# Differential attention: where the band's value weights are split and multiplied, and how its heads are normed

## The chip, the cores and the metric
The kernel runs on one core of a Trainium2 chip. The metric is the device time of one execution in microseconds. It was timed three times; the median counts.

## The reference, cut to what matters
One block of a network on 512 tokens of width 1024: layer norm, a mixer of two attentions with gates, a mixture of 32 experts, and a second block of the same kind. The change touches the first mixer alone.

```python
def diff_attention(q, k, v, lam, lam_init, subln_w):      # 4 heads, two score maps each, values of width 128
    ...
        p = jax.nn.softmax(jnp.where(allowed, s + bias, -jnp.inf), axis=-1)
        a = p[0] - lam * p[1]
        return jnp.einsum('bhqk,bhkd->bhqd', a.astype(v.dtype), v)
    ...
    o = rms_norm(o, subln_w) * (1.0 - lam_init)
    return o.reshape(B, S, WIDTH_A)

    out_a = diff_attention(qa, ka, va, lam, lam_init, subln_w)
    out_b = chunk_band_attention(qb, kb, vb, rel_bias)
    merged = gates[:, :, 0] * (out_a @ w_branch_a) + gates[:, :, 1] * (out_b @ w_branch_b)
```
All of `qa` to `vb` are columns of `h @ w_in`. `rms_norm` works over the 128 values of one head.

## The kernel before, in words
The program is a list of stages. In a stage each engine has its own instructions and the engines meet by counting semaphores; at a stage's end all engines meet (a border). 512 tokens are 4 rows of 128 partitions (`NT`), the width of 1024 is 8 tiles of 128 (`NK`). Every product with weights is made of three TensorE products of 32-bit operands (`split_product`, lines 137 to 139): the weights are cast to an upper part (`fp32r`) by ScalarE, and `split_lower` (line 144) subtracts it from the raw weights on VectorE or GpSimd.

The stages around the change:
- `opening_stage` norms the input, makes the differential values and the projections of the first unit.
- `diff_heads` (`heads_stage`, 4 units of 4 items, numbered t = 0 to 15). An item is 128 queries against 128, 256, 384 or 512 keys. In step t TensorE makes the scores of item t and a piece of the next unit's projections (`projection`; units 2 and 3 are split inside the stage, GpSimd making the lower parts), then turns the weights of item t−2 (`TURN_LAG`) and multiplies values for item t−3 (`VALUE_LAG`). VectorE adds the bias of item t (line 649), and scales item t−1 (lines 680 to 686); ScalarE copies the turned weights of item t−2 out of PSUM (line 720) and takes the exponentials of item t (line 736). The last unit projects nothing. When a unit closes, VectorE copies its 128 columns to `oa` (line 3480). Steps 16 to 18 only finish the last items. SP (the DMA queue) loads the weights of a unit when the projections of an earlier one are done, and with `following` (`band_values`) loads the band's 2 MB of value weights into `ahead` once all projections are done.
- `diffnorm` (`transpose_heads_stage`) does two things at once. The heads: VectorE squares all of `oa` (line 1065), sums (1072), ScalarE takes the root (1108), VectorE the reciprocal (1080) and scales all of `oa` in one operation (1084); TensorE turns it by 16 transposes (1140), ScalarE copies each of the four tiles out of PSUM with the weight column (1114), and VectorE casts and splits each (1090, 144). The band's values for rows 0 and 1 of 4: ScalarE casts the weights by four parts (1105), VectorE makes four lower parts (144), and TensorE multiplies 48 products, 36 ahead of the transposes and 12 behind them; ScalarE copies the two banks out (1120). SP loads the weight column and the band's bias table.
- `bandbias` is a stage of one memset on VectorE (line 761), after the table has landed.
- `band_heads` (`heads_stage` again): SP loads its first weights, TensorE makes 48 products for value rows 2 and 3, then the projections of the first unit, then items as above.

Then come the merge, the output, the routing and the experts, none of which the change touches. Loads of later stages are issued when a semaphore of earlier work allows it.

Of the kernel before, what the change touches and what calls it, by code (L numbers as in the profile page):

```python
# [16 lines left out]
P = 128  # L17
# [554 lines left out]
def attention_pe(nc, pe, k, items, b, projection, opened):  # L572

    N, at = items.n, b["at"]
    for t in range(N + VALUE_LAG):
        if t < N:
# [13 lines left out]
            if not items.closes(t):  # L590
                projection(u + 1, items.place(t))
        n = t - TURN_LAG
# [41 lines left out]
def attention_dve(nc, dve, k, items, b, next_keys, copy_out, ordered, other):  # L634

    N, at = items.n, b["at"]
    for t in range(N + VALUE_LAG + 1):
# [59 lines left out]
        if t < N:  # L697
            other(items.unit(t), items.place(t))
        n = t - VALUE_LAG
        if 0 <= n < N and items.closes(n):  # L700
# [4 lines left out]
            copy_out(u).then_inc(b["out_copied"], 2 if items.mixed else 1)  # L705


def attention_act(nc, act, k, items, b, weights, next_queries, copy_out):

    N, at = items.n, b["at"]  # L710
    for t in range(N + VALUE_LAG + 1):
# [15 lines left out]
        if t < N:  # L727
# [11 lines left out]
            weights(items.unit(t) + 2, items.place(t))  # L739
        n = t - VALUE_LAG  # L740
# [12 lines left out]
def band_bias_stage(nc, k, table):  # L753

    with Stage(nc, "bandbias") as st:
        block = st.block()

        @block.vector
        def _(dve):
            dve.wait_ge(k.band_table_in, 16)  # L760
            nc.vector.memset(table[0:HD, :, S - HD:S], NEG)
# [12 lines left out]

def heads_stage(nc, name, k, load, projections, items, values, q, copy_out, upper_out=None, keys=None, following=None,
                projected_values=False, first=None, beside=None,
                opened=False, prepare=None):
# [4 lines left out]
    with Stage(nc, name) as st:  # L782
# [39 lines left out]
        def _(sp):  # L822
            for u in range(split, units):
# [21 lines left out]
        def _(pe):  # L845
# [42 lines left out]
            attention_pe(nc, pe, k, items, b, projection, opened)  # L888

        @block.scalar  # L890
        def _(act):
# [5 lines left out]

            def weights(u, step):
                if beside is not None and u == 2 and step == 0:
                    upper_part(1, 0)  # L900
# [37 lines left out]
            attention_act(nc, act, k, items, b, weights, next_queries, upper_out)  # L938

        @block.vector  # L940
        def _(dve):
# [20 lines left out]

            def remainders(u, step):
                if beside is not None and u >= 1 and step in (3, 5):
# [5 lines left out]
            attention_dve(nc, dve, k, items, b, next_keys, copy_out, keys is not None and upper_out is not None, remainders)  # L970
# [4 lines left out]
                    v_hi=NT if early else 0, v_ps=len(v_rows), v_sb=len(v_rows))  # L975
# [41 lines left out]
def transpose_heads_stage(nc, name, k, o, o_t, heads=0, weight=None, eps=LN_EPS, factor=1.0, ahead=None, values=None,  # L1017
                          next_upper=None):

    width = o.shape[2]
    tiles = width // P
    n, t0 = k.heads.done["ready"], k.heads.done["transposed"]
    with Stage(nc, name) as st:
# [2606 lines left out]
```

## Time and profile before

| | us |
|---|---|
| median of 3 runs | 2034.96 (2034.91 to 2036.11) |
| profiled execution, its own time | 2034.65 |
| its span | 2032.8 |
| mean granted TensorE clock | 0.981 of full speed |
| TensorE busy | 1933.8 (95%) |
| VectorE busy | 1574.0 (77%) |
| ScalarE busy | 1231.0 (61%) |
| GpSimd busy | 296.8 (15%) |

The differential stage runs from 60 to 130 us of the span, the norm stage to 150, the band from 151. In the rows a line is start, duration, engine, line of the kernel, operation, output<-inputs with shapes; in square brackets stands the engine's idle time before it and what ended it. PE is TensorE, DVE VectorE, ACT ScalarE, POOL GpSimd, SP the DMA queue; "PEq L83" is the border of a stage. Where neighbouring instructions overlap, the distance from start to start is the pace. PEclk is the granted clock of TensorE, 1.00 for 2.4 GHz and 0.50 for 1.2 GHz.

### The profile page before, as it was taken

Reading aid. Unit: us, or ns where it says so; the run is one execution under the profiler, and the core shown is the slowest. Engines: PE = TensorE matmul, PEld = TensorE weight load, DVE = VectorE, ACT = ScalarE, POOL = GpSimd, SP = SyncE. Lnnn points to the kernel's source line nnn. Section 1 sums busy time; section 2 is a strip of 40 time slices with the busy share of each in tenths; the row PEclk is TensorE's granted clock in tenths of the full one; section 3 lists DMA queues with packets and bytes.
Section 4 is the critical chain, followed back from the end, with each engine's and each line's share of the span. In section 5 each row is a group of like instructions: output and inputs, shape, how many; then the busy total and the mean of one; then the engine's idle time right before and its main releaser. Section 6 shows DMA issues by size and latency. Waiting matters only on the chain. (4 is left out here: it accounts for less than half of the span.)

```text
span 2032.8 us, 28745 instructions
## 1 busy us (share of the span) xinstructions
PE 1933.8 (95%) x10074; PEld 1550.4 (76%) x10074; DVE 1574.0 (77%) x1778; ACT 1231.0 (61%) x1319; POOL 296.8 (15%) x172
## 2 busy tenths in 40 slices
PE   6979899989999999999999999999999898899898
PEld 5657678766888888888888888888888685587776
DVE  6662451479999999999999999999999865754787
ACT  3443522326777777777777777777777534753551
POOL 0102044101112111111211121111212100000100
PEclk9989999998999999999999999999999998999999
DMA  6223133539999999999999999999999752011222
GB/s 212 69 84 83 43 98 98 181 135 372 353 392 378 395 374 393 385 384 393 377 392 375 393 384 385 387 382 390 378 396 373 255 110 76 17 37 63 63 65 82
DMA packets 201788, 518.44 MB, mean 255 GB/s; under 512 B 22118, under 2 KB 81678, under 8 KB 201372
## 3 DMA queue, kind: packets, MB, share of 16 engines
q1 hardware_dynamic: 191532, 482.70, 63.9%
q0 software_dynamic: 9360, 34.08, 6.4%
q8 instruction: 41, 0.67, 0.1%
q10 hardware_dynamic: 832, 0.80, 0.1%
q14 instruction: 23, 0.19, 0.0%
HBM read 494.43 MB, written 28.88 MB: 257 GB/s over the span
## 5 line engine op out<-in xcount | busy, mean ns | idle before, releaser
L1991 PE MATMUL bank<-moe_upper,x_hi 128*128 128x512 f32 x1504 | 603.4, 401 | 0.0
L1993 PE MATMUL bank<-moe_upper,x_hi 128*128 128x512 f32 x1504 | 585.9, 390 | 0.0
L2212 DVE TENSOR_TENSOR beyond_lower<-beyond,moe_upper 128x2048 fp32r<-128x2048 f32 x192 | 434.7, 2285 | 32.4 <-ACT moe_upper L2114 32.4
L2114 ACT CAST moe_upper<-beyond 128x2048 fp32r<-128x2048 f32 x192 | 367.6, 1915 | 141.4 <-PE bank L1993 136.8
L1991 PEld LDWEIGHTS bank<-moe_upper,x_hi 128*128 128x128 f32 x1504 | 282.8, 188 | 62.4 <-issue 0.3
L1993 PEld LDWEIGHTS bank<-moe_upper,x_hi 128*128 128x128 f32 x1504 | 282.3, 188 | 59.7
L1992 PE MATMUL bank<-beyond_lower,x_hi 128*128 128x512 f32 x752 | 293.0, 390 | 0.0
L2212 DVE TENSOR_TENSOR mixed_t_lower<-mixed_t,moe_upper 128x2048 fp32r<-128x2048 f32 x96 | 218.2, 2286 | 27.0 <-ACT moe_upper L2114 26.9
L2114 ACT CAST moe_upper<-above 128x2048 fp32r<-128x2048 f32 x96 | 183.6, 1914 | 72.9 <-PE bank L1993 72.9
L2212 DVE TENSOR_TENSOR above_lower<-above,moe_upper 128x2048 fp32r<-128x2048 f32 x96 | 218.1, 2285 | 6.3 <-ACT moe_upper L2114 6.3
L2114 ACT CAST moe_upper<-mixed_t 128x2048 fp32r<-128x2048 f32 x96 | 183.8, 1916 | 58.0 <-PE bank L1993 56.1
L1992 PEld LDWEIGHTS bank<-beyond_lower,x_hi 128*128 128x128 f32 x752 | 141.4, 188 | 28.1
L1992 PE MATMUL bank<-mixed_t_lower,x_hi 128*128 128x512 f32 x376 | 146.8, 390 | 0.0
L1992 PE MATMUL bank<-above_lower,x_hi 128*128 128x512 f32 x376 | 146.3, 389 | 0.0
L1939 POOL COPY moe_dst<-row 128x1 uint32 (+1 forms) x31 | 26.6, 858 | 596.0 <-ACT y L2103 596.0
L139 PE MATMUL bank<-x_hi,ahead_lower 128*128 128x512 f32 x264 | 103.1, 391 | 0.0
L1941 POOL DMA_INDIRECT mixed<-y,moe_dst x31 | 85.0, 2742 | 26.7 <-issue 26.7
L1992 PEld LDWEIGHTS bank<-above_lower,x_hi 128*128 128x128 f32 x376 | 70.6, 188 | 14.6
L1992 PEld LDWEIGHTS bank<-mixed_t_lower,x_hi 128*128 128x128 f32 x376 | 70.9, 188 | 13.5
L1283 DVE TENSOR_TENSOR merge_tmp<-merge_sig,bank 128x512 f32<-128x512 f32 x8 | 5.5, 687 | 81.0 <-PE bank L139 80.6
L1931 POOL COPY moe_tok<-token 128x1 uint32 (+1 forms) x32 | 24.8, 775 | 288.2 <-DMA mixed<-y,moe_dst 268.7
L1933 POOL DMA_INDIRECT ahead<-h,moe_tok x32 | 58.0, 1813 | 26.9 <-issue 26.9
(632 smaller groups left out, 3413.5 us busy)
## 6 DMA issues: line engine op xcount, KB each, us to landing
beyond<-in_w_exp_in_dram SPq DMA_DIRECT2D x128, 1024.0 KB, 8.1
mixed_t<-in_w_exp_in_dram SPq DMA_DIRECT2D x64, 1024.0 KB, 8.1
above<-in_w_exp_in_dram SPq DMA_DIRECT2D x64, 1024.0 KB, 8.1
beyond<-in_w_exp_out_dram SPq DMA_DIRECT2D x64, 1024.0 KB, 9.5
mixed_t<-in_w_exp_out_dram SPq DMA_DIRECT2D x32, 1024.0 KB, 7.6
above<-in_w_exp_out_dram SPq DMA_DIRECT2D x32, 1024.0 KB, 9.4
ahead<-in_w_in_dram SPq DMA_DIRECT2D x23, 512.0 KB, 5.4
ahead<-in_w_in_dram SPq DMA_DIRECT2D x3, 1536.0 KB, 6.7
```

The lines of the kernel that those rows point to most:

```text
L139: return nc.tensor.matmul(out, lhs.lo, rhs.hi, start=False, stop=stop)
L1283: nc.vector.tensor_tensor(tmp[:, :], sig[:, 0, :], k.bank[2][:, :], ALU.mult)
L1931: nc.gpsimd.tensor_copy(tok[:, p:p + 1], r.token[:, ds(j, 1)])
L1933: nc.gpsimd.indirect_dma_start(out=rows_in[p][:, :], out_offset=None, in_=k.h1[:, :], in_offset=bass.IndirectOffsetOnAxis(ap=tok[:, p:p + ...
L1939: nc.gpsimd.tensor_copy(dst[:, :], r.row[:, ds(j, 1)])
L1941: nc.gpsimd.indirect_dma_start(out=k.mixed[:, :], out_offset=bass.IndirectOffsetOnAxis(ap=dst[:, 0:1], axis=0), in_=y[:, :], in_offset=Non ...
L1991: nc.tensor.matmul(to, hi[:, f, :], upper[u][:, t, cols], start=f == 0 and not biased, stop=False)
L1992: nc.tensor.matmul(to, hi[:, f, :], lower[s][:, t, cols], start=False, stop=False)
L1993: done = nc.tensor.matmul(to, lo[:, f, :], upper[u][:, t, cols], start=False, stop=f == NK - 1)
L2114: nc.scalar.copy(upper[h % SPLIT][:, :, :], ring[s][:, :, :]).then_inc(hi_ready, 1)
L2212: nc.vector.tensor_tensor(lower[s][:, :, :], ring[s][:, :, :], upper[h % SPLIT][:, :, :].bitcast(F32), ALU.subtract).then_inc(lo_ready, 1)
```

## The change
- The band's value weights are loaded in two halves of 1 MB: tiles 4 to 7 at the start of `diff_heads`, ahead of unit 2's weights, and tiles 0 to 3 where all 2 MB were loaded before. The weight column is loaded behind them, in `diff_heads`.
- Inside `diff_heads`: ScalarE casts all four parts (2 and 3 in units 0 and 1, 0 behind the last item's exponentials, 1 in step 16), VectorE makes lower parts 2 and 3 (units 0 and 1) and 0 (step 16), and TensorE makes the 24 products of tiles 4 to 7 in steps 12, 13, 14, 16 and 17 (`LATER_STEPS`: six, three, three, six, six), into banks 7 and 0.
- VectorE squares and sums a unit's head right after its copy to `oa`; for the third unit in step 16.
- The new `differential_norm_stage` scales the heads by quarters, and TensorE turns each quarter when it is scaled; it makes 12 products ahead of the transposes and 12 behind them, with lower part 1 made there.
- The stage `bandbias` is gone: its memset and a drain come behind the first key copy of `band_heads`.

```diff
@@ attention_pe
+        if spare is not None:
+            spare(t - N + items.per_unit)
         n = t - TURN_LAG
@@ attention_dve
         if t < N:
             other(items.unit(t), items.place(t))
+        elif spare is not None:
+            spare(t - N)
...
             copy_out(u).then_inc(b["out_copied"], 2 if items.mixed else 1)
+            if summed is not None and u != items.units - 2:
+                summed(u)
@@ attention_act
             weights(items.unit(t) + 2, items.place(t))
+        elif spare is not None:
+            spare(t - N)
@@
-def band_bias_stage(nc, k, table):
...
+def band_bias(nc, k, table, dve):
+
+    dve.wait_ge(k.band_table_in, 16)
+    nc.vector.memset(table[0:HD, :, S - HD:S], NEG)
+    dve.drain()
@@
+LATER_BANKS, LATER_ORDER = (7, 0), (2, 3, 0, 1)
+LATER_STEPS = {0: ((0, 4), (0, 5)), 1: ((0, 6),), 2: ((0, 7),), 4: ((1, 4), (1, 5)), 5: ((1, 6), (1, 7))}
+
+
+def load_later(sp, k, weights, half):
+
+    part = slice(NK // 2 * half, NK // 2 * half + NK // 2)
+    sp.dma_start(k.ahead[:, part, :], weights[:, part, :]).then_inc(k.ahead_in, 16)
+    k.ahead_loads += 16
@@ heads_stage
         @block.sync
         def _(sp):
+            if later is not None:
+                load_later(sp, k, later.weights, 1)
             for u in range(split, units):
...
-            attention_pe(nc, pe, k, items, b, projection, opened)
+
+            def later_products(step):
+                if step == 4:
+                    pe.wait_ge(b["biased"], b["at"] + items.n - 1)
+                for i, c in LATER_STEPS.get(step, ()):
+                    if c % 2 == 0:
+                        pe.wait_ge(v_lo, v0 + c // 2 - 1)
+                    split_product(nc, k.bank[LATER_BANKS[i]][:, :], k.x_parts[:, c, i * P:(i + 1) * P], v_w[:, c, :],
+                                  c == NK // 2, False)
...
+            def later_upper(h):
+                if h == 2:
+                    act.wait_ge(k.ahead_in, ahead_loads + 16)
+                elif h == 0:
+                    act.wait_ge(k.ahead_in, ahead_loads + 32)
+                part = slice(2 * h, 2 * h + 2)
+                nc.scalar.copy(v_upper[:, part, :], k.ahead[:, part, :]).then_inc(v_hi, 1)
+
+            def last_upper(step):
+                if step == 0:
+                    later_upper(1)
+
             def weights(u, step):
+                if later is not None and u in (2, 3) and step == 1:
+                    later_upper(u)
+                if later is not None and u == units + 1 and step == STEPS - 1:
+                    later_upper(0)
...
+            def squares(u):
+                part = later.heads[:, :, u * P:u * P + P]
+                dve.drain()
+                nc.vector.tensor_tensor(later.squares, part, part, ALU.mult)
+                dve.drain()
+                nc.vector.tensor_reduce(later.sums[:, :, u], later.squares, AX.X, ALU.add)
+
+            def last_lower(step):
+                if step == 0:
+                    squares(units - 2)
+                    later_lower(0)
+
             def remainders(u, step):
+                if later is not None and u < 2 and step == 2:
+                    later_lower(u + 2)
@@ differential_norm_stage, in place of transpose_heads_stage
         @block.sync
         def _(sp):
+            ahead(sp)
 
         @block.vector
         def _(dve):
+            nc.vector.tensor_scalar(sums[:, :, :], sums[:, :, :], 1.0 / P, LN_EPS, ALU.mult, ALU.add).then_inc(sum_ready, 1)
+            dve.wait_ge(weight_in, 16)
+            nc.vector.tensor_scalar(wcol[:, :], wcol[:, :], 1.0 - LAM_INIT, None, ALU.mult).then_inc(weight_ready, 1)
+            split_lower(nc.vector, k.ahead[:, 2:4, :], k.v_upper[:, 2:4, :], v_w.lo[:, 2:4, :]).then_inc(v_lo, 1)
+            dve.wait_ge(std_ready, 1)
+            nc.vector.reciprocal(sums[:, :, :], std[:, :, :])
+            dve.drain()
+            for c in range(NT):
+                part = o[:, :, c * P:c * P + P]
+                nc.vector.tensor_tensor(part, part, sums[:, :, c].unsqueeze(2).to_broadcast([P, NT, P]), ALU.mult)\
+                    .then_inc(scaled if c < NT - 1 else ready, 1)
+            for c in range(NT):
+                dve.wait_ge(tile_out, c + 1)
+                nc.vector.tensor_copy(o_t.hi[:, c, :], out[:, c, :])
                 dve.drain()
+                split_lower(nc.vector, out[:, c, :], o_t.hi[:, c, :], o_t.lo[:, c, :])
...
         @block.tensor
         def _(pe):
+            def value_products(i, h):
+                for c in (2 * h, 2 * h + 1):
+                    last = split_product(nc, k.bank[LATER_BANKS[i]][:, :], k.x_parts[:, c, i * P:(i + 1) * P],
+                                         v_w[:, c, :], False, c == NK // 2 - 1)
+                return last
+
+            pe.wait_ge(v_lo, lo0 + 3)
+            for i in range(2):
+                value_products(i, 0)
+            for c in range(NT):
+                if c < NT - 1:
+                    pe.wait_ge(scaled, c + 1)
+                else:
+                    pe.wait_ge(ready, 1)
                 for i in range(NT):
...
+            pe.wait_ge(v_lo, lo0 + 4)
+            for i in range(2):
+                value_products(i, 1).then_inc(v_ps, 1)
@@ program
             def band_values(sp):
-                load_ahead(sp, k, column_tiles(A["w_in"][0], 5 * WA, 512))
+                load_later(sp, k, later.weights, 0)
+                with nc.allow_non_contiguous_dma(reason="a column of weights"):
+                    sp.dma_start(later.wcol[:, :], A["subln_w"].rearrange("o p -> p o")).then_inc(k.heads["weight_in"], 16)
...
-            band_bias_stage(nc, k, band_table)
...
-                lambda m: None, band_lower, band_upper, following=merge_early, projected_values=True)
+                lambda m: None, band_lower, band_upper, following=merge_early, projected_values=True,
+                prepare=lambda dve: band_bias(nc, k, band_table, dve))
```

## Rows read from the trace of the kernel before
**Rows 1.** The page of the profile, its first line.
```profile
span 2032.8 us, 28745 instructions
```

**Rows 2.** Busy time by stage: window, its length, busy time of each engine, clock, DMA.
```profile
60.00:110.90 50.90, 49.89 (x251) 36.82 (x251) 28.00 (x92) 21.65 (x61) 9.44 (x4) 1.00 0.21 62
110.90:129.20 18.30, 13.77 (x80) 9.66 (x79) 12.97 (x46) 9.24 (x27) 0.00 (x0) 0.91 0.33 116
129.20:133.77 4.57, 0.00 (x0) 0.00 (x0) 4.17 (x4) 3.50 (x4) 0.00 (x0) 0.71 0.43 102
133.77:144.01 10.24, 10.24 (x37) 8.22 (x37) 8.32 (x8) 1.88 (x3) 0.00 (x0) 0.80 0.42 159
...
148.70:151.15 2.45, 0.00 (x0) 0.03 (x1) 1.64 (x4) 0.58 (x1) 0.00 (x0) 1.00 0.00 0
151.15:163.76 12.61, 12.61 (x49) 10.26 (x49) 0.00 (x0) 2.48 (x3) 4.75 (x2) 0.86 0.32 84
```

**Rows 3.** The timeline of VectorE, 129 to 151 us.
```profile
129.28 0.69 DVE L3480 COPY oa<-bank 128x512 f32<-128x512 f32 x1 [3.19 <-PE bank L623]
130.29 2.29 DVE L1065 TENSOR_TENSOR diffnorm_sq<-oa 128x2048 f32<-128x2048 f32 x1 [0.32 <-PEq L83]
132.50 2.35 DVE L144 TENSOR_TENSOR ahead_lower<-ahead,v_upper 128x1024 fp32r<-128x1024 f32 x2
...
135.01 2.29 DVE L1072 TENSOR_REDUCE diffnorm_sums<-diffnorm_sq 128x16 f32<-128x2048 f32 x1
...
138.59 0.24 DVE L1080 RECIPROCAL diffnorm_sums<-diffnorm_std 128x16 f32<-128x16 f32 x1
...
145.43 0.43 DVE L1090 CAST oa_t_upper<-oa_t 128x512 fp32r<-128x512 f32 x1 [3.09 <-ACT oa_t L1114]
...
149.24 0.69 DVE L144 TENSOR_TENSOR oa_t_lower<-oa_t,oa_t_upper 128x512 fp32r<-128x512 f32 x1
...
150.36 0.48 DVE L761 MEMSET band_table<- 64x512 f32 x1 [0.43 <-PEq L83]
```

**Rows 4.** The timeline of ScalarE: a table load, a cast, the evictions.
```profile
11.22 1.28 ACT L187 ACT_TABLE_LOAD   x1
12.51 0.20 ACT L187 ACTIVATE setup_std<-setup_ve 128x4 f32<-128x4 f32 x1
...
73.30 1.04 ACT L896 CAST first_upper<-first_raw 128x1024 fp32r<-128x1024 f32 x1
...
144.70 2.42 ACT L1114 ACTIVATE oa_t<-bank,diffnorm_wcol 128x512 f32<-128x512 f32 x4 [6.91 <-PE bank L1140]
```

**Rows 5.** The timeline of TensorE, 143 to 152 us.
```profile
143.78 0.39 PE L139 MATMUL bank<-v_upper,x_lo 128*128 128x512 f32 x1
144.01 1.91 PE L1140 MATMUL bank<-const,oa 128*128 128x128 f32 x16
...
151.15 0.47 PE L137 MATMUL bank<-v_upper,x_hi 128*128 128x512 f32 x1 [2.47 <-PEq L83]
```

**Rows 6.** The timeline of TensorE in the last unit of the differential stage.
```profile
114.71 0.55 PE L601 MATMUL bank<-const,diff_scores 128*128 128x128 f32 x3 [1.73 <-DVE diff_scores L686]
...
124.28 0.90 PE L601 MATMUL bank<-const,diff_scores 128*128 128x128 f32 x3 [2.00 <-DVE diff_scores L686]
124.97 1.06 PE L623 MATMUL bank<-v,diff_pt 128*128 128x128 f32 x4
126.15 1.11 PE L601 MATMUL bank<-const,diff_scores 128*128 128x128 f32 x4
```

**Rows 7.** The timeline of VectorE and GpSimd, 79 and 115 us.
```profile
79.53 2.95 DVE L686 SCALAR_TENSOR_TENSOR diff_scores<-diff_scores,diff_l 128x512 f32<-128x512 f32 x1
79.57 2.36 POOL L144 TENSOR_TENSOR first_raw_lower<-first_raw,first_upper 128x1024 fp32r<-128x1024 f32 x1 [2.80 <-ACT first_upper L896]
...
115.86 0.75 DVE L686 SCALAR_TENSOR_TENSOR diff_scores<-diff_scores,diff_l 128x512 f32<-128x512 f32 x1
```

**Rows 8.** DMA issues, 55 to 72 us: count, KB each, us to landing.
```profile
first_raw<-in_w_in_dram SPq DMA_DIRECT2D x2, 512.0 KB, 6.7
```

More of the change, by code:

```diff
@@ L937, in _ @@
                     upper_part(1, n)
-            attention_act(nc, act, k, items, b, weights, next_queries, upper_out)
+            attention_act(nc, act, k, items, b, weights, next_queries, upper_out, None if later is None else last_upper)
         @block.vector
@@ L968, in remainders @@
                     split_lower(nc.vector, k.ahead[:, :, part], beside[:, :, part], k.ahead_lower[:, :, part])
-            attention_dve(nc, dve, k, items, b, next_keys, copy_out, keys is not None and upper_out is not None, remainders)
+            attention_dve(nc, dve, k, items, b, next_keys, copy_out, keys is not None and upper_out is not None, remainders,
+                          None if later is None else squares, None if later is None else last_lower)
     k.attention.counted(scored=items.n, out_copied=2 * units)
@@ L1044, in _ @@
         def _(sp):
-            if heads:
-                with nc.allow_non_contiguous_dma(reason="a column of weights"):
-                    sp.dma_start(wcol[:, :], weight).then_inc(weight_in, 16)
-            if ahead is not None:
-                ahead(sp)
+            ahead(sp)
         @block.vector
         def _(dve):
-            if next_upper is not None:
-                for m in range(4):
-                    part = slice(P * m, P * m + P)
-                    dve.wait_ge(next_hi, m + 1)
-                    split_lower(nc.vector, k.ahead[:, :, part], next_upper[:, :, part], k.ahead_lower[:, :, part])
@@ L1117, in _ @@
-            if values is not None:
-                for i in range(2):
-                    act.wait_ge(v_ps, i + 1)
-                    nc.scalar.copy(values[:, i, :], k.bank[4 + i][:, :])
+            act.wait_ge(sum_ready, 1)
+            nc.scalar.activation(std[:, :, :], sums[:, :, :], ACT.Sqrt).then_inc(std_ready, 1)
+            act.wait_ge(weight_ready, 1)
+            for c in range(NT):
+                act.wait_ge(transposed, c + 1)
+                nc.scalar.activation(out[:, c, :], k.bank[NORM_TURNED + c][:, :], ACT.Copy, scale=wcol[:, 0:1])\
+                    .then_inc(tile_out, 1)
@@ L1141, in _ @@
                 last.then_inc(transposed, 1)
-            if values is not None:
-                value_products(3)
-    k.heads.counted(transposed=tiles, ready=1 if heads else 0)
+            pe.wait_ge(v_lo, lo0 + 4)
+            for i in range(2):
+                value_products(i, 1).then_inc(v_ps, 1)
+    k.units.counted(v_lo=1)
+    k.heads.counted(transposed=NT, ready=1)
 def load_merge(sp, w_in, branches, raw, f, loaded):
@@ L3476, in program @@
                 first = first_raw, first_lower, first_upper
+                later = Kernel()
+                later.weights, later.heads = column_tiles(A["w_in"][0], 5 * WA, 512), oa[:, :, :]
+                later.sums = s2.enter_context(nc.sbuf_tensor("head_sums", [P, NT, NT], F32))[:, :, :]
+                later.squares = oa_t.whole[:, 0, :].rearrange("p (i d) -> p i d", d=P)
+                later.wcol = s2.enter_context(nc.sbuf_tensor("head_weight", [P, 1], F32))
                 opening_stage(nc, k, A, table, first)
```

135 lines of the change are left out of this document (31 added, 104 removed).

## Prediction, made before the changed kernel ran

> **What bounds the kernel now.** I read first the span [rows 1]; the profiled execution took 2034.65 us, 1.85 us more than it, and the median of the three runs is 2034.96 us, 0.31 us above. So what I take off the span comes off both, and the median stands 0.31 us above the profiled one. Then I cut the stretch around the change by stage and asked for busy time and clock [rows 2]. Three things are to be seen. Up to 110.9 us TensorE is busy 49.9 of 50.9 us: it is the bound, and VectorE (28.0) and ScalarE (21.7) have room. From 110.9 to 129.2 us, the last unit of differential attention, nobody is full: TensorE 13.8 of 18.3 us, a chain that goes round the engines. Then TensorE does nothing for 4.57 us, works 10.24 us at a granted clock of 0.80, and after the stage does nothing for 2.45 us; the 48 products that open the band stage take 12.61 us at 0.86.
>
> Third, the timeline of each engine there. VectorE's [rows 3] shows the norm stage as a staircase: the last `oa` copy at 129.28, squares, two `lower` parts, the sums, the scaling, and from 145.43 to 149.93 four casts with their remainders, then a stage for one memset at 150.36. TensorE's [rows 5] shows the transposes at 144.01, behind 36 products, and the band at 151.15. From VectorE's first instruction of the norm stage to TensorE's first of the band it is 151.15 − 130.29 = 20.86 us.
>
> **The norm stage, after.** I count from its first VectorE instruction, T, at which TensorE begins too.
> - ScalarE: table load 1.28 and square root 0.20 [rows 4], with nothing ahead of them now (the four casts are gone): 1.5 us.
> - VectorE: the two small operations (0.08 apart, 0.3 with the issue) and one `lower` part (2.35 for two, 1.2 each) [rows 3]: also 1.5. The reciprocal with its gap, 0.3–0.4 [rows 3], to 1.9. Four quarter scalings at the price of a 128x512 tensor_tensor, 0.69, some 0.61 from start to start [rows 3]: the first is ready at 2.6, the last at 4.45.
> - TensorE: 12 products before the transposes instead of 36, at 0.23 each (143.78 to 144.01 [rows 5]) 2.75, so the first transpose starts at 2.85, just after the first quarter is scaled.
> - From first transpose to first cast passed 144.01 to 145.43, 1.42 [rows 3, 5]: 4.3; VectorE is free at 4.45. So the casts start at 4.45, and they took 4.5 us for all four: 8.95. TensorE's other 12 products end at about 7.5 and their evictions (0.6 each, as the four of 2.42 [rows 4]) at about 8.5, beside them.
> - One border, 0.32 (129.97 to 130.29 [rows 3]), and no stage for the memset: TensorE starts the band at 9.3.
>
> Gain: 20.86 − 9.3 = **11.55 us**. The memset of 0.48 us moves behind VectorE's key copy in the band. The first scores wait on TensorE for that copy too, and the second item's come microseconds of projections later; if the cover were gone it would cost 0.5. I take 0.
>
> **What goes into the differential stage.** Each piece, and what hides it:
> - 24 products move to the last unit. At 0.23 us, the six at its first item (1.4) fit the 1.73 us in which TensorE waited before 114.71, and the six of step 4 (1.4) fit the 2.00 us before 124.28 [rows 6]. The three and three between have 0.3 us of idle: they push the next scores, which VectorE (13.0 of 18.3 us busy [rows 2]) takes up in part. I book 0.4, about half of the 0.7 that three products last. The last six come directly ahead of the last item's transposes (126.15), a chain without idle: 1.4 us. Against it, the stretch from 124.28 ran at the lower level (0.91 for the unit as a whole [rows 2]); with the idle filled I expect 2.4 GHz, by which the 3 transposes and 4 value products (124.28 to 126.03) take 0.9 instead of 1.75, and the rest up to the copy some 0.5 less. So: 0.4 + 1.4 − 0.85 − 0.5, about 0.4 us on `oa`'s last copy. Bounds: nothing, and 3.1 if the clock stays low and the six take twice as long.
> - Head squares and sums. A pair costs 0.69 and 0.65 (a quarter of the 2.29 of the reduction [rows 3], with its overhead) and drains: 1.4. Units 0 and 1 have it while TensorE projects; unit 2's comes with `lower` 0 (1.2) after VectorE's last scaling (the transposes that wait for it start at 126.15 [rows 6]), 2.6 us in the 3.19 us that it idles before 129.28 [rows 3]. Unit 3's has no cover: the stage ends with it, **1.4 us**. Bounds 1.2 and 1.6.
> - `lower` parts 2 and 3 on VectorE, four casts of 1.04 on ScalarE [rows 4]: the first two on either engine in units 0 and 1, where TensorE is the bound. The last two casts lie behind the last exponentials and between the last copies of transposed scores: TensorE is behind its six products by then. 0.
> - SP: half the value weights (1 MB) now go ahead of unit 2's weights, and the rest behind the projections, 1 MB instead of 2. Unit 2's two landed 6.7 us after their issue at 60.06 [rows 8], and are cast at 73.30 [rows 4]: 6.5 us of slack. Another 1 MB, at what these two took, is 6.7 at the very most; I expect it hidden, bounds 0 and 0.5. The weight column is loaded earlier; the band's table is issued first in the norm stage and is needed at the memset, over 20 us on.
>
> So the differential stage ends 1.8 us later (at 131.8 against 129.97).
>
> **The band's start.** TensorE stood still 2.45 us before 151.15, and the products behind ran at 0.86 [rows 2]. 48 at 0.23 are 10.95 us, against 12.61: 1.65 us lost to the lower level. After the change TensorE ends its products at T + 7.5 and goes on at T + 9.3: 1.8 us, or less. Rows of the same unit: 1.73 us idle before 114.71 was followed by products of unchanged pace, 2.00 before 124.28 by slower ones [rows 6]. 1.8 lies between, nearer 1.73: I take the clock as kept, **−1.65 us**; the other bound is 0.
>
> **Sum.** 2034.65 − 11.55 + 1.8 − 1.65 = 2023.25 us; on the median of the runs, **2023.6 us**. Behind the band's start each piece is shifted alike, since its loads are issued by progress, not by time.
>
> **Two rules against the trace.** ScalarE's table load at 11.22 is followed by an activation at 12.51, 1.29 us on [rows 4]: nothing is lost beyond the load's 1.28. The Trainium skill, "ScalarE: Activation LUTs", What ACT_TABLE_LOAD costs, gives a switch 1283 ns plus a drain of about 1380 ns. The rule would put the square root, and with it all of VectorE's staircase, 1.3 us later; the trace of before does not agree with it. VectorE's 128x512 scalar_tensor_tensor at 79.53 took 2.95 us, begun as GpSimd's split of 2.36 us ran; at 115.86, with GpSimd idle, it took 0.75 [rows 7]. The Trainium skill, "SBUF — State Buffer", on the shared port pair, has it that an operation with two SBUF inputs and one of GpSimd exclude each other for the whole instruction; the trace agrees with that, and the new squares and `lower` parts are such operations.
>
> **Rivals.**
> - *The clock falls.* TensorE idles about 2.5 us before T (4.57 before less the 3.48 that it waited inside the stage, and the 1.4 of the sums), and 2.00 and 2.45 us were followed by the lower level. The 10.24 us at 0.80 hold 4.1 us at the lower level, in which only nine of the 36 products fit [rows 2], 0.45 each. Most of the 12 products at that, 5.1 in all: the transposes start at 5.2 and the stage lasts 11.6: 2.3 us lost; with the band's start low too, 1.65 more; with the tail at its bound, 2.7 more. 2025.9, 2027.6 or 2030.3 us. For it: the gap is in the range that brought it. Against: the tail, now denser, counts beside it. 0.30.
> - *The table switch costs more than its row*, by 1.3: the scalings end at 5.75 and the casts with them: 2024.9 us. 0.04.
> - *VectorE collides with GpSimd* in the differential stage: 2.2 us each time (2.95 − 0.75). There are seven new two-input operations there (four squares, three `lower` parts); the splits are four, and TensorE's projections cover units 0 and 1. All seven on the path would cost 15.4, to 2039.0 us, slower. It decides from the seventh collision on; before it only eats the gain. 0.02.
> - *The gain is given back*, by a load or a clock further down: within 0.2%, above 2030.9 us. 0.04.
> - *More is gained*, below 2021.8 us: the tail wholly hidden and a quarter of a stage besides. 0.05.
> - The forecast, 2021.8 to 2025 us: 0.55.
>
> **Range and chances.** About 0.2% (4.1 us) is what a measurement of this kernel can tell from no change. The low end is the sum with the tail's 1.8 hidden; the high end is the clock rival without its last term and with a microsecond more: 2021.8 to 2028.6. Faster 0.94, within 0.2% 0.04, slower 0.02.
>
> **What would show it.** In the profile after: six products each in the gaps before the transposes of the 11th and the 15th of the sixteen items; the last `oa` copy within a microsecond of 129.3; squares and a sum after it; a norm stage of about 9 us with the first transpose 2.9 us in, VectorE without a wait from the scalings to the last remainder; clock 1.00 in it and in the band's first 11 us. Wrong would be: a clock of 0.5 there, TensorE waiting for ScalarE's casts in the tail, or a late table load.

## The result, and the profile after

The changed kernel takes 2022.49 us (median of 4 runs, 2020.8 to 2025.76) against 2034.93 us: a ratio of 0.9936, 95% interval 0.9916 to 0.9956, and 12.4 us less. The forecast was 2023.6 us, in a range of 2021.8 to 2028.6. The profiled execution took 2023.78 us, 10.9 below that of the kernel before. So the total came out as forecast; the stretch around the change did not quite, and that is what the rest is about.

The stages once more, cut at the same events as in [rows 2] (columns as there):
```profile
60.00:110.70 50.70, 49.89 (x251) 36.84 (x251) 32.94 (x98) 23.40 (x63) 9.45 (x4) 1.00 0.28 83
110.70:129.35 18.65, 17.64 (x103) 12.43 (x103) 15.59 (x49) 10.93 (x29) 0.00 (x0) 1.00 0.19 57
129.35:132.03 2.68, 0.03 (x1) 0.03 (x1) 2.07 (x3) 0.04 (x1) 0.00 (x0) 0.82 0.00 0
132.03:137.28 5.25, 5.25 (x12) 4.04 (x13) 4.11 (x8) 1.47 (x2) 0.00 (x0) 0.50 0.79 265
...
142.24:143.80 1.56, 0.00 (x0) 0.03 (x1) 1.19 (x3) 0.59 (x1) 0.00 (x0) 1.00 0.00 0
143.80:154.80 11.00, 11.00 (x48) 9.09 (x49) 0.00 (x0) 2.48 (x3) 3.37 (x2) 1.00 0.36 98
```
The last unit of the differential stage is now nearly full of TensorE work, 17.6 of 18.7 us (13.8 of 18.3 before), at a clock of 1.00 instead of 0.91, and it is only 0.35 us longer. Where 36 products took 10.24 us ahead of the transposes, there are now 12, but these take 5.25 us, since the clock is at 0.50 for all of them. The band's first 48 products run at 1.00 and take 11.00 us instead of 12.61.

VectorE, as in [rows 3]:
```profile
126.58 0.69 DVE L1014 TENSOR_TENSOR oa_t<-oa 128x512 f32<-128x512 f32 x1
127.34 0.69 DVE L1016 TENSOR_REDUCE head_sums<-oa_t 128x4 f32<-128x512 f32 x1
127.95 1.22 DVE L144 TENSOR_TENSOR ahead_lower<-ahead,v_upper 128x1024 fp32r<-128x1024 f32 x1
129.49 0.69 DVE L3501 COPY oa<-bank 128x512 f32<-128x512 f32 x1 [0.33 <-PE bank L625]
130.27 0.69 DVE L1014 TENSOR_TENSOR oa_t<-oa 128x512 f32<-128x512 f32 x1
131.04 0.69 DVE L1016 TENSOR_REDUCE head_sums<-oa_t 128x4 f32<-128x512 f32 x1
132.03 0.18 DVE L1104 TENSOR_SCALAR head_sums<-head_sums 128x16 f32<-128x16 f32 x1 [0.30 <-PEq L83]
...
133.87 2.50 DVE L1113 TENSOR_TENSOR oa<-oa,head_sums 128x512 f32<-128x512 f32 x4
139.00 0.43 DVE L1117 CAST oa_t_upper<-oa_t 128x512 fp32r<-128x512 f32 x1 [2.63 <-ACT oa_t L1128]
...
142.81 0.69 DVE L144 TENSOR_TENSOR oa_t_lower<-oa_t,oa_t_upper 128x512 fp32r<-128x512 f32 x1
```
The square, the sum and the `lower` part at 126.58 stand in what was an idle stretch; the last copy to `oa` starts at 129.49 (129.28 before); the square and the sum behind it, to 131.73, stand alone. The norm stage begins at 132.03. The four quarter scalings are over at 136.4, and then VectorE waits 2.63 us for the first turned tile, which the forecast had ready when VectorE was free. The remainders end at 143.50, and TensorE's next line shows the band 0.30 us later.

TensorE, as in [rows 5] and [rows 6]:
```profile
124.66 0.55 PE L603 MATMUL bank<-const,diff_scores 128*128 128x128 f32 x3 [0.78 <-DVE diff_scores L688]
...
126.87 0.60 PE L603 MATMUL bank<-const,diff_scores 128*128 128x128 f32 x4
...
132.03 0.77 PE L137 MATMUL bank<-v_upper,x_hi 128*128 128x512 f32 x1 [2.65 <-PEq L83]
132.59 0.63 PE L138 MATMUL bank<-ahead_lower,x_hi 128*128 128x512 f32 x1
133.02 0.63 PE L139 MATMUL bank<-v_upper,x_lo 128*128 128x512 f32 x1
...
137.28 2.20 PE L1151 MATMUL bank<-const,oa 128*128 128x128 f32 x16
...
143.80 0.47 PE L137 MATMUL bank<-v_upper,x_hi 128*128 128x512 f32 x1 [1.57 <-PEq L83]
```
The gap before the 15th item's transposes is 0.78 instead of 2.00 us: six products fill it, and 124.66 runs at the full pace (0.55 for the three transposes that took 0.90). TensorE then stands still for 2.65 us ahead of 132.03, and the products behind are 0.43 us apart (132.59 to 133.02) instead of 0.23. Ahead of 143.80 it stands still for 1.57 us, and what follows is at the full pace.

ScalarE's table load, as in [rows 4]:
```profile
132.00 1.28 ACT L1124 ACT_TABLE_LOAD   x1 [3.82 <-PEq L83]
133.29 0.22 ACT L1124 ACTIVATE diffnorm_std<-head_sums 128x16 f32<-128x16 f32 x1
```
The root follows 1.29 us behind the load's start. The drain of about 1.38 us that the Trainium skill, "ScalarE: Activation LUTs", What ACT_TABLE_LOAD costs, adds to each load does not show here either.

### The profile page after: what moved, and what is told of

Same layout as the page of the kernel before. It is cut to its first block and busy times, and to the rows that moved or that the text cites. A ratio compares the mean times of both kernels' runs of the same rounds, so it can differ in the third digit from the quotient of the medians.

```text
span 2022.0 us, 28752 instructions
## 1 busy us (share of the span) xinstructions
PE 1930.3 (95%) x10074; PEld 1546.7 (76%) x10074; DVE 1576.5 (78%) x1787; ACT 1230.7 (61%) x1319; POOL 291.1 (14%) x172
## 5 line engine op out<-in xcount | busy, mean ns | idle before, releaser
L139 PEld LDWEIGHTS bank<-x_hi,ahead_lower 128*128 128x128 f32 x264 | 49.6, 188 | 10.8
```

The costliest lines, as they stand in the source:

```text
L139: return nc.tensor.matmul(out, lhs.lo, rhs.hi, start=False, stop=stop)
```

## The experiments

Run times scatter more than the edits are worth: on the chips of the experiments the kernel before itself ran from 2030.4 to 2043.8 us. So each run is read on one stretch of its trace, from the differential stage's last key copy to the band's first, which every kernel has in the same places. The two rows that bound it in the changed kernel:
```profile
110.71 0.69 DVE L989 COPY diff_heads_kt<-bank 128x512 f32<-128x512 f32 x1 [0.45 <-PE bank L139]
...
165.88 0.69 DVE L989 COPY band_heads_kt<-bank 128x512 f32<-128x512 f32 x1 [10.19 <-PE bank L139]
```
The same differences for all, in us (T is VectorE's first instruction of the norm stage; the last column is the stretch between the two key copies; each is worked out from the starts in that kernel's timelines):

| kernel | key copy to T | T to first transpose | T to the band's first product | its 48 products | key copy to key copy |
|---|---|---|---|---|---|
| before | 19.35 | 13.72 | 20.86 | 12.61 | 63.90 |
| changed | 21.32 | 5.25 | 11.77 | 11.00 | 55.17 |
| after_again | 21.31 | 5.26 | 11.76 | 11.00 | 55.15 |
| after_third | 21.32 | 4.42 | 10.65 | 10.98 | 54.03 |
| fill_gap | 21.50 | 2.84 | 9.06 | 11.00 | 52.64 |
| early_products | 21.83 | 2.59 | 9.98 | 10.98 | 53.87 |
| early_fill | 21.83 | 2.58 | 9.05 | 11.00 | 52.96 |
| six_last | 21.04 | 2.81 | 9.05 | 11.00 | 52.16 |
| six_last_again | 21.05 | 2.82 | 9.05 | 10.96 | 52.14 |
| whole_scaling | 21.32 | 4.41 | 10.63 | 11.00 | 54.03 |
| sums_in_norm | 19.78 | 7.08 | 15.14 | 10.98 | 56.98 |
| products_in_norm | 20.96 | 9.65 | 15.87 | 11.00 | 58.91 |
| bias_inside | 19.36 | 13.83 | 20.06 | 11.00 | 61.50 |
| before_fill | 19.46 | 11.78 | 18.91 | 11.00 | 60.45 |

**The changed kernel again, twice** (no edit).

> The changed kernel once more, for a second trace and a fair spread. Theory (the gap sets the clock): TensorE's still time of about 2.6 us ahead of the norm stage is followed by the lower level, so the 12 products take about 5.1 us and the first transpose starts 5.2 us into the stage, as in the first trace; where the lower level ends may differ, and with it the runs scatter by 2 to 3 us, which those of the kernel before (1.5 us) do less. Rival (the products are slow for another reason, such as the 2 MB table load beside them): they take 5.1 us in every trace at a granted clock of 1.00. About 2022.5 us.

> The changed kernel a third time, as the neighbour of the next one. By the two traces so far the stretch from the last key copy of the differential stage to the first of the band is 55.2 us (63.9 in the kernel before), of which 2.5 us are the 12 products at the lower level. Theory: 55.2 again, or 52.6 where the lower level should miss them; the whole scatters by 2 us or more with the clock of other stretches.

2021.49 us (2019.67 to 2026.47) and 2023.85 us (2020.52 to 2027.91); ratios to the kernel before 0.9941 (0.9922 to 0.9959) and 0.9943 (0.9921 to 0.9964). The second trace repeats the first within 0.02 us; in the third the lower level came a little later and left sooner, 1.1 us better. So the 12 products are slow in each of the three traces, by an amount that varies with where the lower level begins and ends. The expectation that the kernel before scatters less was wrong: beside these runs it went from 2030.42 to 2040.38.

**fill_gap**: TensorE is given something to do in the gap.
```diff
             attention_pe(nc, pe, k, items, b, projection, opened, None if later is None else later_products)
+            if later is not None:
+                fill(nc, k, 5, 11)      # 11 products of x_hi with itself into bank 5, which nobody reads
```


> The changed kernel with 11 more products of no use on TensorE at the end of the differential stage, 0.23 us each, so that it is busy to the border. Theory (the gap sets the clock): the granted clock stays 1.00 through the norm stage, the 12 products take 2.75 us instead of 5.2, the first transpose starts at 2.9 us, the first cast is set by VectorE at 4.45 us, and the band starts 9.3 us into the stage instead of 11.8: 2.3 to 2.5 us less, about 2020 us, with less scatter. Rival (another reason): the 12 products keep 0.43 us each and the time stays at 2022.5 us. Second rival (the 11 products delay the border): up to 0.3 us of the gain is lost.

TensorE's timeline (line 156 is the filler):
```profile
129.31 2.78 PE L156 MATMUL bank<-x_hi 128*128 128x512 f32 x11
132.39 0.47 PE L137 MATMUL bank<-v_upper,x_hi 128*128 128x512 f32 x1 [0.30 <-PEq L83]
132.70 0.39 PE L138 MATMUL bank<-ahead_lower,x_hi 128*128 128x512 f32 x1
132.93 0.40 PE L139 MATMUL bank<-v_upper,x_lo 128*128 128x512 f32 x1
...
135.24 2.20 PE L1159 MATMUL bank<-const,oa 128*128 128x128 f32 x16
```
The gap is 0.30 us, the products are 0.23 us apart, and the first transpose starts 2.84 us in. The stage is 2.7 us shorter, the border 0.2 later: 52.64 us against 55.17. The table of the band's bias is loaded beside it as before, so it was not that. The stretch thus takes 11.26 us less than in the kernel before, against the forecast's sum of 11.4. The whole shows none of it: 2023.87 us (ratio 0.9944, 0.9927 to 0.9961) against its neighbour after_again's 2021.49, where about 2020 was expected. Its trace has more of the lower level elsewhere than that of after_again (from 1880 to 1920 us the clock is 0.87 against 1.00), and 2.5 us are less than the scatter.

**early_products and early_fill**: the 12 products ahead of the transposes go into the gap themselves; then fillers where the norm stage waits for its first quarter.
```diff
             attention_pe(nc, pe, k, items, b, projection, opened, None if later is None else later_products)
+            if later is not None:
+                pe.wait_ge(v_lo, v0 + 3)
+                for i in range(2):
+                    for c in (0, 1):
+                        split_product(...)
@@ differential_norm_stage
-            pe.wait_ge(v_lo, lo0 + 3)
-            for i in range(2):
-                value_products(i, 0)
+            fill(nc, k, 6, 9)           # early_fill only
```


> The changed kernel with the 12 products of tiles 0 and 1 moved from the start of the norm stage to the end of the differential one, where TensorE stands still. Theory (TensorE's 12 products at the lower level are what the norm stage waits for): the first transpose starts when the first quarter is scaled, 2.6 us into the stage, the casts follow VectorE's scalings at about 4.5 us, and the band starts 9.3 to 10 us in, whatever the clock; the differential stage ends up to 0.5 us later. 1.5 to 2.3 us below the changed kernel. Rival (ScalarE's or VectorE's staircase is the bound): no change beyond 0.5 us.

> The same, with 9 products of no use on TensorE at the start of the norm stage, where it would wait for the first quarter (2.1 us). Theory: the clock stays at 1.00 to the band's end of value products; the norm stage is VectorE's staircase, 9.3 us; against the kernel without these 9 it wins 0 to 1 us, where its last 12 products or the band's first ones ran at the lower level. Rival: the nine delay the transposes, up to 0.2 us lost.

2024.76 us (0.9952, 0.9934 to 0.9971) and 2024.51 us (0.9952, 0.9934 to 0.9969). The first transpose starts at 2.59 and 2.58 us, when the first quarter is scaled, and the border comes 0.5 us later, both as expected. The gain of early_products is less than expected: its stretch is 1.3 us shorter than the changed kernel's, not 1.5 to 2.3, because TensorE waits 2.88 us for the quarter instead, and the lower level comes there. Its TensorE timeline:
```profile
132.87 0.39 PE L139 MATMUL bank<-v_upper,x_lo 128*128 128x512 f32 x1
136.15 3.42 PE L1154 MATMUL bank<-const,oa 128*128 128x128 f32 x16 [2.88 <-DVE oa L1119]
139.22 0.78 PE L137 MATMUL bank<-v_upper,x_hi 128*128 128x512 f32 x1
```
The transposes take 3.42 us instead of 2.20, the last 12 products end late and their evictions set the end, 9.98 us in. With fillers it is 9.05. The gap had only been moved; of the two, 53.87 and 52.96 us, the second gains 2.2 over the changed kernel and pays 0.5 for the border.

**whole_scaling**: one scaling of all heads instead of four quarters.
```diff
-            for c in range(NT):
-                part = o[:, :, c * P:c * P + P]
-                nc.vector.tensor_tensor(part, part, sums[:, :, c]..., ALU.mult).then_inc(scaled if c < NT - 1 else ready, 1)
+            nc.vector.tensor_tensor(o3, o3, r3, ALU.mult).then_inc(ready, 1)
```


> The changed kernel with the heads scaled by one operation and turned after it, as before. Theory (the 12 products at the lower level end at 5.2 us, so the quarters are ready long before they are used): the scaled heads are ready at 4.2 us instead of a first quarter at 2.6, and nothing moves, 0 to 0.2 us, as long as the clock is low; with a full clock it would cost 1.3 us. Rival (the quarters bring what the norm stage gained): 1.5 us or more longer.

2023.41 us (0.9919, 0.9896 to 0.9943). Its row in the table is that of after_third, which had the lower level in the same place, to 0.02 us: the first transpose at 4.41 and 4.42. The quarters brought nothing there, since the 12 products end later than the whole scaling. That they would bring 1.3 us at a full clock was not measured by itself; fill_gap, with quarters, starts its transposes 2.84 us in, 1.3 us before the 4.12 at which the whole scaling ends here.

**sums_in_norm**: squares and sums of all heads in the norm stage.
```diff
+            nc.vector.tensor_tensor(later.squares, o, o, ALU.mult)
+            dve.drain()
+            nc.vector.tensor_reduce(sums[:, :, :], later.squares..., AX.X, ALU.add)
```


> The changed kernel with squares and sums of all heads back in the norm stage, 2.29 us each. Theory: the differential stage ends 1.4 us earlier, and VectorE's first quarter is scaled at 6.9 us instead of 2.6, so the casts start at about 8.8 instead of 7.0 us (they waited for TensorE): 1.8 minus 1.4, about 0.4 us longer than the changed kernel at a low clock, 2.9 against one at a full clock. Rival (the sums by pair are a gain by themselves): 3 us or more longer.

2027.56 us (0.9942, 0.992 to 0.9964), stretch 56.98. The differential stage ends 1.54 us earlier, the first quarter and the first cast (9.01 us in) come as expected, and yet it is 1.8 us longer than the changed kernel, not 0.4. TensorE, with nothing to do for 4.09 us, was at the lower level for the transposes and the first few of the last products, as its timeline has it:
```profile
138.64 3.67 PE L1147 MATMUL bank<-const,oa 128*128 128x128 f32 x16 [4.09 <-DVE oa L1109]
141.96 0.78 PE L137 MATMUL bank<-v_upper,x_hi 128*128 128x512 f32 x1
...
146.70 0.47 PE L137 MATMUL bank<-v_upper,x_hi 128*128 128x512 f32 x1 [0.92 <-PEq L83]
```
Its evictions then end the stage, 15.14 us in, and not VectorE's remainders at 13.5. So the sums by pair were worth 1.8 us against the first two traces of the changed kernel and 2.95 against the third; how much of it is the clock was not taken apart.

**products_in_norm**: all 48 value products in the norm stage, casts and lower parts where the change put them.
```diff
-            attention_pe(..., opened, None if later is None else later_products)
+            attention_pe(..., opened)
@@ differential_norm_stage
-            pe.wait_ge(v_lo, lo0 + 3)
-            for i in range(2):
-                value_products(i, 0)
+            for h in (2, 3, 0):
+                pe.wait_ge(v_lo, lo0 + (h - 1 if h else 3))
+                for i in range(2):
+                    value_products(i, h)
```


> The changed kernel with all 48 value products in the norm stage; casts and lower parts stay in the differential stage. Theory (TensorE's products are the norm stage's bound): 36 products ahead of the transposes, 8.2 us at the full clock and up to 11 with 5 us at the lower one, so the first transpose at 9 to 11 us instead of 5.2 and the band 3.5 to 5.5 us later within the stage; the differential stage ends 0.4 to 0.5 us earlier. 3 to 5 us longer than the changed kernel. Rival (it was the casts' absence that brought the gain, TensorE's share is hidden): below 2 us longer.

2028.96 us (0.9956, 0.9936 to 0.9977), stretch 58.91: 3.7 us longer, with the first transpose at 9.65 us and the border 0.36 earlier. The 24 moved products are worth 3.7 of the 8.7 us of the stretch, net of the 0.4 that they cost where they went, the largest of the parts undone here. The clock has a share in that too: the 36 products ahead of the transposes ran at the lower level for their first 3 us, the changed kernel's 12 for all 5.25. What it is worth to have ScalarE's four casts out of the norm stage was not measured by itself.

**six_last, twice**: the last six of the moved products behind the last item's value products.
```diff
-LATER_STEPS = {..., 4: ((1, 4), (1, 5)), 5: ((1, 6), (1, 7))}
+LATER_STEPS = {..., 4: ((1, 4), (1, 5)), 7: ((1, 6), (1, 7))}
...
             attention_pe(nc, pe, k, items, b, projection, opened, None if later is None else later_products)
+            if later is not None:
+                later_products(7)
```


> The changed kernel with the last six products inside the differential stage moved from ahead of the last item's transposes to behind its value products. Theory (they stand in a chain without idle): the last copy to oa starts 0.4 to 0.8 us earlier, and so does the norm stage; and TensorE stands still 1.2 us before it instead of 2.6, so the lower level may stay away, 2.3 us more. Between 0.5 and 3 us below the changed kernel. Rival (the six kept the clock up in the tail): the tail falls to the lower level and the last copy is no earlier.

> The kernel with the last six products behind the last item's value products, once more. Theory: the same stretch takes 52.2 us, 3.0 less than the changed kernel (0.3 by the earlier copy, 2.7 by the clock), in this trace too, since TensorE stands still only 1.2 us. Whether the whole time shows it: 0 to 3 us less than its neighbour. Rival (the full clock of the first trace was luck): 54 to 55 us in this one.

TensorE in the second, first its timeline:
```profile
125.12 0.55 PE L603 MATMUL bank<-const,diff_scores 128*128 128x128 f32 x3 [0.77 <-DVE diff_scores L688]
...
127.00 0.66 PE L603 MATMUL bank<-const,diff_scores 128*128 128x128 f32 x4 [0.89 <-DVE diff_scores L688]
...
129.32 0.48 PE L137 MATMUL bank<-v_upper,x_hi 128*128 128x512 f32 x1
```
and its busy time by window (the clock is the third number from the right):
```profile
126.00:129.00 3.00, 2.03 (x17) 1.73 (x16) 2.76 (x5) 2.13 (x4) 0.00 (x0) 1.00 0.00 0
...
130.70:132.20 1.50, 0.27 (x2) 0.02 (x1) 1.14 (x2) 0.02 (x1) 0.00 (x0) 1.00 0.00 0
132.20:141.20 9.00, 7.78 (x40) 6.07 (x40) 8.24 (x16) 5.07 (x8) 0.00 (x0) 1.00 0.68 233
```
Nothing stands between value products and the transposes at 127.00 now, which wait 0.89 us for VectorE: the six had cost the chain 0.28 us, less than the 0.4 expected, because VectorE was the later one. Behind 129.32 stand the six, the gap is 1.25 us (1.5 of the window at 130.7), and the clock is 1.00 throughout. 52.16 and 52.14 us in two traces, 3.0 less than the changed kernel and the best of all. The runs took 2022.62 us (0.9929, 0.9902 to 0.9955) and 2021.18 us (0.9933, 0.9912 to 0.9955). All 10 have a median of 2021.6, all 16 of the changed kernel of 2022.8; an advantage of 1.2 us that these runs do not establish.

**bias_inside and before_fill**, on the kernel before: the memset's stage alone taken away; TensorE's gap of 4.57 us filled.
```diff
-            band_bias_stage(nc, k, band_table)
...
+                prepare=lambda dve: band_bias(nc, k, band_table, dve))
```
```diff
             attention_pe(nc, pe, k, items, b, projection, opened)
+            if opened_early:            # the differential stage
+                fill(nc, k, 5, 4)
@@ transpose_heads_stage
             if values is not None:
+                fill(nc, k, 6, 14)
```


> The kernel before with one edit of the change: the stage of the memset is gone and the memset stands behind the band's first key copy. Theory: one border and the memset, 1.22 us from the last remainder to TensorE's first product, become 0.31: 0.9 us less, and the first scores' bias is not later. Rival (the memset shows in the band): nothing gained.

> The kernel before with 4 products of no use at the end of the differential stage and 14 at the start of the norm stage, where TensorE stands still for 4.57 us. Theory (the gap sets the clock): the 36 products ahead of the transposes run at 0.23 us from about 133.8 us on and take 8.3 us instead of 10.2, so the transposes start at 142.1 instead of 144.0 us: 1.9 us less. Rival (contention with the table load, not the clock): the 36 products still take 10.2 us.

2034.12 us (0.9992, 0.9979 to 1.0006) and 2035.43 us (0.9996, 0.9983 to 1.001), neither apart from the kernel before, whose 23 runs beside them went from 2030.54 to 2041.92. In the traces the first product of the band stands 0.31 us behind the last remainder instead of 1.22 in bias_inside: the 0.9 that was expected. In before_fill the granted clock is 1.00 where it was 0.71 and 0.80 [rows 2]; its windows:
```profile
128.90:133.30 4.40, 4.10 (x18) 2.90 (x16) 3.96 (x3) 3.30 (x4) 0.00 (x0) 1.00 0.35 86
133.30:141.80 8.50, 8.47 (x37) 6.82 (x37) 8.26 (x9) 2.10 (x3) 0.00 (x0) 1.00 0.53 202
```
and the 36 products take 8.3 us, so the transposes start 1.94 us earlier, as the theory has it. Both kernels also have the band's 48 products in 11.00 us instead of 12.61, which was not expected of either: bias_inside with a gap of 1.6 us ahead of them, before_fill with the same gap as the kernel before, as TensorE's timeline there shows:
```profile
148.94 0.47 PE L137 MATMUL bank<-v_upper,x_hi 128*128 128x512 f32 x1 [2.48 <-PEq L83]
```

## Why the prediction was right, and where it was lucky

**The norm stage** (11.55 us forecast). Measured 9.1 (20.86 to 11.77) and, with the gap filled, 11.8 (to 9.06). The steps that go by the work to be done were right to 0.25 us: first transpose at 2.85 (2.84 in fill_gap), casts at 4.45 (4.26), band at 9.3 (9.06). What was off is the term for the 12 products, taken at 0.23 us each; they ran at 0.43. That was named as a rival, at 2.3 us and a chance of 0.30, and it is what came: 2.7 us in the first trace, 2.7 and 1.6 in the others. By the forecast's own sign ("a clock of 0.5 there") this step was wrong. Every gap of 2.0 us and more in [rows 2, 5, 6] was followed by the lower level, and the forecast itself worked out a gap of 2.5 us before T. Yet those rows were not all: the trace of before also has a gap of 2.98 us, ahead of the first scores of the differential stage, behind which the clock stays at 1.00, while in after_third it is 0.50 for the first 6 us behind the gap at the same place, 2.69 us there. The first line is of the kernel before, the second of after_third:
```profile
60.84 0.49 PE L587 MATMUL bank<-diff_heads_kt,diff_heads_q 64*128 64x128 f32 x4 [2.98 <-DVE diff_heads_kt L946]
...
58.70 0.80 PE L587 MATMUL bank<-diff_heads_kt,diff_heads_q 64*128 64x128 f32 x4 [2.69 <-DVE diff_heads_kt L989]
```
So the rows could give a chance and no rule. The step that failed is the choice of the full clock as the likelier one for the 12 products. That standing still brought the lower level at this place is shown from both sides: it came in all five traces with the gap of 2.65 us, and in none of the four in which the gap was filled (fill_gap, early_fill and six_last twice); before_fill shows the same on the kernel before.

**The differential stage** (+1.8 us). Measured from key copy to T: 21.32 against 19.35, +1.97. The sums behind the last copy cost 1.53 (1.4 forecast), and the last copy itself comes 0.44 us later (0.4 forecast). The idle at 124 is filled and the clock there is full, as forecast. But the 0.4 was right by luck, since two of its four terms were off and cancelled. The last item's scaling on VectorE, in the kernel before and in the changed one:
```profile
125.34 0.75 DVE L686 SCALAR_TENSOR_TENSOR diff_scores<-diff_scores,diff_l 128x512 f32<-128x512 f32 x1
...
125.73 0.75 DVE L688 SCALAR_TENSOR_TENSOR diff_scores<-diff_scores,diff_l 128x512 f32<-128x512 f32 x1
```
Counted from the last key copy (110.71, and 110.94 before) it ends 15.77 us in instead of 15.15, so all the work on the way to it, with the products in between, cost 0.6 (0.4 booked), and the 0.85 booked as a gain of the clock behind 124.28 brought nothing on this way. The six products ahead of the last transposes delayed these by another 0.3, not by the 1.4 booked, for TensorE would have waited for VectorE there anyway, 0.89 us in six_last. From the last transposes to the copy it is 2.62 us instead of 3.13, the 0.5 that was booked. The casts and `lower` parts cost nothing that these rows set apart.

**SP's load ahead of unit 2's weights** was hidden, with 3.2 us less to spare. The DMA issues of the changed kernel from 55 to 72 us, and ScalarE's timeline at unit 2's cast:
```profile
first_raw<-in_w_in_dram SPq DMA_DIRECT2D x2, 512.0 KB, 9.9
```
The cast:
```profile
73.09 1.03 ACT L923 CAST first_upper<-first_raw 128x1024 fp32r<-128x1024 f32 x1
```
Unit 2's weights landed 9.9 us after their issue instead of 6.7 [rows 8], 3.2 more; the cast at 73.09 was not late (73.30 before, and the stage began 0.2 us later then). Of 6.5 us of slack some 3 are used.

**The band's start** (−1.65). Measured −1.61: the gap fell to 1.57 us and the 48 products took 11.00. Right; but before_fill had the full clock behind a gap as long as that of the kernel before, so the gap alone does not decide it.

**The collision with GpSimd** did not come, because none of the seven new two-input operations met one of GpSimd's four splits. The nearest is the square of the first head, which is over 0.1 us before a split begins, as the timeline of both shows:
```profile
90.77 0.69 DVE L1014 TENSOR_TENSOR oa_t<-oa 128x512 f32<-128x512 f32 x1
...
91.53 0.69 DVE L1016 TENSOR_REDUCE head_sums<-oa_t 128x4 f32<-128x512 f32 x1
...
91.58 2.37 POOL L144 TENSOR_TENSOR ahead_lower<-ahead,v_upper 128x1024 fp32r<-128x1024 f32 x1 [9.86 <-ACT v_upper L923]
```
The reduction behind it, with one input, ran beside the split and was not held up: 0.69 us. That agrees with the Trainium skill, "SBUF — State Buffer", on the shared port pair, which has a VectorE operation with two SBUF inputs contend with GpSimd. What a new square would lose beside a split, no run here shows.

**The rest.** Forecast −11.4 in all; the stretch gave −8.73 and the whole profiled run −10.87. 0.2 us of the difference lies ahead of the key copy, 1.9 behind the band's first one. One place of it was found: TensorE's work in the band's last items ran at 0.64 before and at 1.00 after. The window of the kernel before:
```profile
243.30:248.00 4.70, 4.69 (x34) 3.72 (x34) 1.05 (x3) 2.73 (x6) 0.00 (x0) 0.64 0.02 3
```
and of the changed one:
```profile
234.40:239.00 4.60, 4.25 (x50) 3.39 (x50) 1.05 (x3) 2.52 (x6) 0.00 (x0) 1.00 0.02 4
```
Nothing was changed there, and both kernels have the same gap of 1.59 us ahead of it. The distance between the two kernels' traces is 8.9 us at VectorE's second key copy of the band (209.42 and 200.50) and 10.1 at its first operation of the merge (278.27 and 268.19), so some 1.2 us of the 1.9 lie here; the rest was not tracked further. The medians differ by 12.4 us, 1.6 more than the two profiled executions, and no trace shows where. So 2023.6 was near 2022.5 in part by luck: a term taken 2.7 us too good met 2 us of gain, and in the medians 3.7, that no term of the forecast explains.

## What to carry to other kernels

Before taking a clock level for the work behind a border, add up how long TensorE stands still on both sides of the border, and look for the same gap in more than one trace: here 2.65 us of standing still nearly doubled the price of the next 12 products in the first trace, while a gap of 2.98 us elsewhere cost nothing in the kernel before. Filling the gap at the border with useful products (six of them, from a place where they stood in the chain) did as well as filling it with useless ones. When a sum comes out right, check its terms one by one: one error of 2.7 us and a cancelling pair of 1.1 and 0.85 us do not show in a total that is 1.1 us off. And where edits are worth 1 to 3 us and runs scatter by more, compare one stretch between two events that all kernels have, and claim for the whole only what its runs show.

## What the runs showed of the hardware

TensorE's granted clock behind a gap, by place:
- *Ahead of the norm stage.* A gap of 2.65 us was followed by the lower level in all five traces that have it (changed, after_again, after_third, whole_scaling and products_in_norm), but from different moments and for different times: the first transpose came 5.25 or 4.4 us in for the same 12 products.
- *Ahead of the 15th item's transposes.* A gap of 2.0 us was followed by it in all four traces that have it (before, bias_inside, before_fill and products_in_norm). With six products in it, 0.78 us was left and the clock stayed full.
- *Ahead of the band.* A gap of 2.5 us was followed by it in the kernel before and not in before_fill. Gaps of 0.9 to 1.6 us there were not, in any trace.
- *Near the band's end.* The same gap of 1.59 us was followed by it in the kernel before (the stretch at 243.30 above starts behind it) and not in the changed kernel.
- *Ahead of the differential stage's first scores*, behind 16 us and more of products without a pause, all fourteen traces have a gap of 2.6 to 3.0 us. In three the products behind it began at the lower level (after_third, early_products and sums_in_norm), in two it came about 1.7 us into them (whole_scaling and six_last_again), and in nine it did not come. From the stage's first key copy to its second it is 17.2 to 17.4 us in those three, 16.0 in the two and 14.5 in the nine. This lies ahead of all the edits of the experiments, so up to 2.9 us of a difference between two profiled executions can come from here alone.

So neither the length of a gap nor the program decides the level by itself, and the same kernel does not have one time: on the chips of the experiments the kernel before spread over 13 us, far more than its four first runs (1.5 us) had suggested. How much of that spread is the clock was not measured run by run.
